# An adaptive-norm router that reads raw rows, and one point of interleaved work moved ahead of the next expert turn's gather

## The reference, cut to what matters

```python
mod = cond @ w_ada + b_ada
shift1, scale1, gate1, shift2, scale2, gate2 = jnp.split(mod, 6, axis=-1)
x = x + gate1[:, None, :] * hybrid_mixer(h, ...)          # 256 x 1024
h = rms_norm(x, norm2_w) * (1 + scale2[:, None, :]) + shift2[:, None, :]
logits = h @ w_router + b_router                          # 256 x 32
top_v, top_e = lax.top_k(logits, 4); gates = softmax(top_v)
# rows of h are sorted by expert; for each expert e in use:
y_e = clamped_swiglu(h[rows_e] @ w1[e] + b1[e]) @ w2[e] + b2[e]
x = x + gate2[:, None, :] * sum over a row's experts of gate * y
```

## Time and profile before

| what | value |
|---|---|
| median of 3 runs (lowest, highest) | 2353.44 us (2350.11, 2357.47) |
| the profiled execution's own time | 2354.66 us |
| its span | 2353.0 us |
| mean granted TensorE clock (share of full speed) | 0.973 |
| busy share: PE, DVE, ACT, POOL | 92%, 59%, 28%, 7% |
| moved by DMA | 713.89 MB, mean 303 GB/s |
| chain that ended last: PE, DMA, DVE, ACT, issue | 67%, 14%, 13%, 2%, 2% |

### The profile page before, as it was taken

One profiled execution on the slowest core, in us unless ns is written; L12 is line 12 of the kernel. 1 busy time (PEld: TensorE's weight loads), 2 busy tenths in 40 slices (PEclk: granted clock), 3 DMA queues, 4 the chain that ended last, 5 costly groups with the idle time before them and its releaser, 6 DMA issues.

```text
span 2353.0 us, 40321 instructions
## 1 busy us (share of the span) xinstructions
PE 2156.2 (92%) x16516; PEld 1507.4 (64%) x16516; DVE 1378.7 (59%) x2660; ACT 659.5 (28%) x832; POOL 170.2 (7%) x229
## 2 busy tenths in 40 slices
PE   6998989988998998888998889899989999998998
PEld 5897843444544445445544555677769888876987
DVE  2466454534453444565544455877678676678876
ACT  1332120212222221211111111444443334455332
POOL 1320010000000000000000000000000000020000
PEclk8999989999999999999999999999999999999999
DMA  9889879998999999999999999554446533334652
GB/s 382 309 324 353 322 294 386 420 419 362 419 419 419 407 420 419 419 410 419 404 419 419 409 404 403 199 174 166 167 145 213 183 137 119 108 117 159 209 187 72
DMA packets 112031, 713.89 MB, mean 303 GB/s; under 512 B 12624, under 2 KB 13280, under 8 KB 36912
## 3 DMA queue, kind: packets, MB, share of 16 engines
q1 hardware_dynamic: 86048, 616.93, 66.4%
q0 software_dynamic: 25808, 94.48, 10.7%
HBM read 705.06 MB, written 4.19 MB: 301 GB/s over the span
## 4 chain that ended last, share of the span: by engine, by line
PE 67%; DMA 14%; DVE 13%; ACT 2%; issue 2%; POOL 0%; SPq 0%; DVEq 0%; ACTq 0%
PE bank L326 17%; PE bank L2366 6%; PE bank L2347 6%; PE bank L2094 4%; PE bank L2132 4%; DMA hT<-in_panels_e 3%; PE bank L2247 3%; DMA cst<-in_panels_e 3%; DMA ring<-in_units_a 2%; PE bank L2295 2%; PE bank L2480 2%; PE bank L1589 2%; DMA hid<-in_panels_e 2%; PE bank L1755 2%; DMA craw<-in_panels_m 2%
## 5 line engine op out<-in xcount | busy, mean ns | idle before, releaser
L326 PE MATMUL bank<-hid,scratch 128*32 128x512 f32 x1008 | 306.3, 606 | 7.8 <-DMA hT<-in_panels_e 4.3
L326 PE MATMUL bank<-hT,scratch 128*32 128x512 f32 x976 | 301.2, 608 | 12.9 <-DMA hT<-in_panels_e 11.5
L1343 ACT CAST chi<-craw 128x1024 fp32r<-128x1024 f32 x128 | 133.7, 1045 | 544.0 <-DMA craw<-in_panels_m 203.7
L3400 DVE TENSOR_TENSOR clo<-craw,chi 128x1024 fp32r<-128x1024 f32 x128 | 156.0, 1221 | 156.1 <-ACT chi L1343 155.1
L326 PE MATMUL bank<-rows,scratch 128*32 128x512 f32 x632 | 172.1, 601 | 8.0 <-DMA cst<-in_panels_e 7.2
L326 PE MATMUL bank<-diag_gtmp,scratch 128*32 128x512 f32 x648 | 177.2, 600 | 2.0 <-DMA hid<-in_panels_e 1.5
L326 PE MATMUL bank<-cst,scratch 128*32 128x512 f32 x632 | 175.6, 603 | 3.0 <-DMA yacc<-in_panels_e 3.0
L326 PE MATMUL bank<-yacc,scratch 128*32 128x512 f32 x648 | 174.0, 595 | 2.5 <-DMA diag_gtmp<-in_panels_e 2.5
L2094 PE MATMUL bank<-cT_hi,chi 128*128 128x256 f32 x384 | 113.3, 295 | 17.2 <-DVE cT_lo L3319 5.5
L326 PEld LDWEIGHTS bank<-hT,scratch 128*32 128x32 f32 x976 | 70.5, 111 | 66.0 <-issue 65.5
L2094 PE MATMUL bank<-cT_lo,chi 128*128 128x256 f32 x384 | 110.3, 287 | 0.0
(11 more groups left out here) (721 smaller groups left out, 5813.5 us busy)
## 6 DMA issues: line engine op xcount, KB each, us to landing
hid<-in_panels_e SPq DMA_DIRECT2D x96, 1024.0 KB, 12.8
hT<-in_panels_e SPq DMA_DIRECT2D x94, 1024.0 KB, 13.4
ring<-in_units_a SPq DMA_DIRECT2D x70, 1024.0 KB, 7.8
ring<-in_panels_m SPq DMA_DIRECT2D x64, 1024.0 KB, 5.1
yacc<-in_panels_e SPq DMA_DIRECT2D x48, 1024.0 KB, 12.4
diag_gtmp<-in_panels_e SPq DMA_DIRECT2D x48, 1024.0 KB, 13.8
rows<-in_panels_e SPq DMA_DIRECT2D x47, 1024.0 KB, 13.1
cst<-in_panels_e SPq DMA_DIRECT2D x47, 1024.0 KB, 12.7
```

The lines of the kernel that those rows point to most:

```text
L326: m = self.pe.matmul(b[s:s + STRIP, :], lhs(k)[:, s:s + STRIP], v, start=(first and k == 0), stop=(k == KT - 1))
L1343: act.copy(chi[:, h % 2, :], context_raw(h)).then_inc(cx_hi, 1)
L3400: tt(context_lower(h), context_raw(h), chi[:, h % 2, :], ALU.subtract).then_inc(cx_lo, 1)
```

## The change

*Raw rows.* The norm's scale is multiplied into the router's weights `wr` and the router's product with the shift is added to its bias `brow`, both while the mixer still runs. TensorE transposes `tok` itself, ScalarE copies the banks out unscaled, and VectorE multiplies the summed logits by `rstd` and adds `brow`. The upper part of the normed rows is made by ScalarE from `tok` and `rstd` (so `xn` is not made), the lower part by VectorE in four pieces (`lower_rows`). *First bias.* Its loads no longer wait for `b1_go`; ScalarE's copy (after `b1_go`) and GpSimd's subtraction come before the router. *First gather.* `first_gather` takes the four products with `xr_hi` first, and turned gates come after the gathered rows; a turn's first product starts after half of the gathered rows, its second half panel after all. *Loads.* One half panel is issued between two ring units, not after the rows are ready. *Turns.* On VectorE `beside(9)` stands ahead of `weights` and `gathered`.

```diff
@@ ScalarE: first bias, rows
-            act.sem_inc(rowp.free, 2)
...
-                    m = act.activation(hT[:, k, t * P:t * P + P], b[:, (k % 4) * P:(k % 4) * P + P], ACT.Identity,
-                                       scale=scol[:, 0, k:k + 1], bias=scol[:, 1, k:k + 1])
...
+            act.wait_ge(filled, B1_FILLED)
+            act.wait_ge(b1_in, 32)
+            act.wait_ge(b1_go, 1)
+            act.copy(b1t[:, :], b1raw).then_inc(b1_upper, 1)
...
+            def row_columns(t, c):
+                act.wait_ge(rows_turned, 2 * t + c + 1)
+                act.copy(hT[:, 4 * c:4 * c + 4, t * P:t * P + P], bank[2 * t + c][:, :].rearrange("p (k n) -> p k n", k=4))\
+                    .then_inc(rows_out, 1)
...
-                act.copy(xr_hi[:, t, :], xn[:, t, :]).then_inc(upper_ready, 1)
+                act.activation(xr_hi[:, t, :], tok[:, t, :], ACT.Copy, scale=rstd[:, t:t + 1]).then_inc(upper_ready, 1)
@@ SyncE
-            for n in range(late + 2, late + 4):
-                first_unit(n, UNIT)
-            first_panel(rows_ready, XT, 1, 0)
+            first_unit(late + 2, UNIT)
+            half_panel(pe_[1], load_of(-1, 1, 1), 1)
+            first_unit(late + 3, UNIT)
+            sp.wait_ge(rows_ready, XT)
+            half_panel(pe_[1], load_of(-1, 1, 0), 0)
@@ GpSimd
-            pool.wait_ge(b1_go, 1)
...
-            for t in range(XT):
-                pool.wait_ge(upper_ready, FRONT_PARTS + t + 1)
-                pool.tensor_tensor(xr_lo[:, t, :], xn[:, t, :], xr_hi[:, t, :], ALU.subtract).then_inc(lower_in, 1)
-            pool.wait_ge(lower_in, FRONT_PARTS + XT)
+            pool.wait_ge(b1_in, 32)
@@ TensorE: shift through the router, ahead of the level chain; into the bias, between two features
+            S.close(partial_sums(b, router, lambda k: scol[:, 1, k:k + 1], range(KT)))
...
+            S.close(pe.matmul(b[:, 0:EXPERTS], shift_part.to_broadcast([P, P]), stack[:, :], start=True, stop=True))
@@ TensorE: router
+            for t in range(XT):
+                for c in range(2):
+                    from_dve.get()
+                    for k in range(4):
+                        m = pe.transpose(bank[2 * t + c][:, k * P:k * P + P], tok_part(t, 4 * c + k), ident)
+                    m.then_inc(rows_turned, 1)
...
@@ TensorE: first gather
+                pieces = [(xr_hi, t, c) for c in range(2) for t in range(XT)]
+                pieces += [(xr_lo, 0, 0), (xr_lo, 0, 1), (xr_lo, 1, 0), (xr_lo, 1, 1)]
...
-            gather()
-            turn_gates()
+            first_gather()
             turn_gathered(0)
             turn_gathered(1)
-            S.read()
+            turn_gates()
@@ TensorE: first product of a turn
-                EA.read()
+                EA.read(1)
@@ VectorE: fold
+            scales(0, 3, {0: (parcol[:, 8:16], None)}, (0,))
...
+            S.done(copy(shift_part, b[:, 0:1]))
+            S.settle()
+            tt(wr[:, :, :], wr[:, :, :], scol[:, 0, :].unsqueeze(2).to_broadcast([P, KT, EXPERTS]), ALU.mult)
...
+            S.done(tt(brow[:, :], brow[:, :], b[:, 0:EXPERTS], ALU.add))
...
@@ VectorE: lower rows, logits
+                stt(xr_lo[:, t, s], tok[:, t, s], rstd[:, t:t + 1], xr_hi[:, t, s], ALU.mult, ALU.subtract).then_inc(lower_in, 1)
...
-                to_tensor.send(ts(xn[:, t, :], tok[:, t, :], rstd[:, t:t + 1], None, ALU.mult))
...
+                m = stt(lg[:, t, :], b[:, EXPERTS * t:EXPERTS * t + EXPERTS], rstd[:, t:t + 1], brow[:, :], ALU.mult, ALU.add)
...
@@ VectorE: an expert turn
                 second(0)
+                beside(9)
                 dve.wait_ge(EA.pair.full, EA.c.at(1))
                 weights(following, shares)
                 gathered(0)
                 gathered(1)
                 if last:
                     added_so_far()
-                beside(9)
```

More of the change, by code:

```diff
@@ L1947, in _ @@
             rows_product(1)
[L1949 to L1961, removed]
-            b = S.open()
[L1963 to L1970, removed]
-            R.read()
-            partial_sums(b, router, cols[1], range(4))
-            S.read()
-            S.close(partial_sums(b, router, cols[1], range(4, KT)))
-            b = S.open()
-            pe.matmul(b[:, 0:EXPERTS], logit_part[:, 0, :], stack[:, :], start=True, stop=True)
-            S.read()
-            S.close(pe.matmul(b[:, EXPERTS:2 * EXPERTS], logit_part[:, 1, :], stack[:, :], start=True, stop=True))
+            for t in range(XT):
[4 more added lines that the diff above has]
+                    m.then_inc(rows_turned, 1)
+            for t in range(XT):
+                b = A.open()
+                for c in range(2):
+                    pe.wait_ge(rows_out, 2 * t + c + 1)
+                    m = partial_sums(b, router, lambda k: hT[:, k, t * P:t * P + P], range(4 * c, 4 * c + 4))
+                A.close(m)
+            b = S.open()
+            for t in range(XT):
+                A.read(XT - 1 - t)
+                m = pe.matmul(b[:, EXPERTS * t:EXPERTS * t + EXPERTS], logit_part[:, t, :], stack[:, :], start=True, stop=True)
+            S.close(m)
             ada_product(AD)
@@ L2007, in _, with first_gather @@
             from_experts = Post(pe, E["to_pe"])
+            def first_gather():
+                pe.wait_ge(upper_ready, FRONT_PARTS + XT)
+                EA.read()
+                pe.wait_ge(EH.pair.free, 2)
+                pieces = [(xr_hi, t, c) for c in range(2) for t in range(XT)]
+                pieces += [(xr_lo, 0, 0), (xr_lo, 0, 1), (xr_lo, 1, 0), (xr_lo, 1, 1)]
+                for n, (piece, t, c) in enumerate(pieces):
+                    if n >= 4:
+                        pe.wait_ge(lower_in, FRONT_PARTS + n - 3)
+                    m = pe.matmul(EH.pair.banks[c][:, :], OH[:, t, :], piece[:, t, 512 * c:512 * c + 512],
+                                  start=(n in (0, 2)), stop=(n >= 6))
+                    if n >= 6:
+                        EH.close(m)
             def gather():
@@ L2030, in first_product @@
                 for h in range(2):
+                    if h and j == 0:
+                        EA.read()
                     EG.rows(b, lambda k: xg[:, k, :], False, h)
@@ L2144, in expert_turn @@
                     pe.wait_ge(b2_in, 16)
+                    S.read()
                     AD.read()
@@ L3076, in _ @@
                     m = gated_rows(c, t)
+                    if t and not c:
+                        lower_rows(0, 0)
                 ask_roots(m, (t,), center=False, eps=EPS_RMS)
                 roots_in((t,))
[L3079 removed]
                 dve.memset(idle[:, 1:2], 0.0).then_inc(rows_ready, 1)
+            for t in range(XT):
+                b = A.take()
+                A.done(copy(logit_part[:, t, :], b[:, 0:P]))
             b = S.take()
[L3082 to L3092 removed]
+            for t in range(XT):
+                m = stt(lg[:, t, :], b[:, EXPERTS * t:EXPERTS * t + EXPERTS], rstd[:, t:t + 1], brow[:, :], ALU.mult, ALU.add)
+            S.done(m)
             S.settle()
```

60 lines of the change are left out of this document (27 added, 33 removed).

## The result

The changed kernel takes 2342.89 us (median of 9 runs, 2335.81 to 2351.32) against 2353.44 (9 runs, 2350.11 to 2359.65): ratio 0.9941, 95% interval 0.9928 to 0.9954, so about 14 us less with 11 and 17 as bounds. The ratio is the one on record and is not that of the two medians, which differ by 10.6 us (0.9955); the two means differ by 12.0. The gain is therefore known to a few microseconds only. The forecast was 2341, within 2335 to 2349, a gain of 12.7. The profiled execution has a span of 2339.7.

A forecast was written before the change was run, and what follows sets the result against it. The cross-engine chain before the first expert product, then the weight stream, bound the kernel. Start 7.3, turn 1 3.9 and turn 9 1.5 sum to 12.7 us, from 2354.66 (2342.0) or median 2353.44 (2340.7): 2341, range 2335 to 2349.

The forecast's parts named there:

- A: From the end of the mixer's output product to the router's logits: 10.5 us becomes 5.8, gain 4.7.
- B: From the logits to VectorE's read of the counts: gain 3.2 us, with GpSimd's subtraction moved away and the counts ending last.
- E: From the first gather matmul to the first expert product: 7.04 us becomes 5.5 to 5.6, gain 1.5.
- the pair: VectorE's two 128x32 gate-scaling instructions, 4.46 us before, would fall to near 0.5 once clear of GpSimd's subtraction.
- Ahead of T0: Before the mixer's output product ends (T0): norm scale and shift folded into the router cost 2.1 us, 0.8 to 2.6.
- C: From the read of the counts to the one-hots and first gather matmul: unchanged at 2.47 us.
- Rival 4: TensorE's low clock through router and gather gives 2343.3, or GpSimd's moved subtraction 2346.5; chance 0.66 shared with the sum.
- D: Lower halves of the normed rows: four VectorE subtractions replace GpSimd's two, covered by upper gather matmuls to within 0.2 us.
- rival 1: Weight stream takes the earlier start back, with panel waits up to 380 us: 2349.3, or 2348 by the median; chance 0.12.
- The tenth point: Expert turns, VectorE's crot_lo made ahead of next turn's rows: gain 3.9 us in turn 1, 1.5 in turn 9.
- Rival 2: In turn 1 the wait at the tenth point only moves and stays as long: 2345.9 us; chance 0.12.
- Rival 3: Next turn's gathered rows come late at turn ends, so TensorE waits: slower, 2365 us; chance 0.06.

The follow-up runs named there:

- the changed kernel once more: The changed kernel measured a second time without any edit: ratio 0.9926 (0.9904 to 0.9947), median 2342.40 us.
- the full read: Changed kernel with a turn's first product waiting again for all eight gathered-row instructions: 2350.39 us, one time only.
- both points ahead: Changed kernel with the eleventh point ahead of one-hots and gathered rows and the fourth ahead of the places for the next experts: ratio 0.9928.
- the later start: Changed kernel with ten repeats of one lower-rows operation on VectorE ahead of the one-hots, changing no value: ratio 0.9978 (0.9964 to 0.9992).
- the first bias late: Changed kernel with ScalarE's first-bias copy, and so GpSimd's subtraction, back behind the exponentials: ratio 0.9950 (0.9931 to 0.9968).
- the tenth point alone: Kernel before with only `beside(9)` moved ahead of the next turn's one-hots and gathered rows: ratio 0.9976 (0.9962 to 0.9991).
- the eleventh point ahead: Changed kernel with `beside(10)` too moved ahead of the one-hots and gathered rows: 2351.99 us in one execution; also run with the fourth point moved, ratio 0.9928.
- the front alone: Changed kernel with the tenth point put back behind the one-hots and gathered rows: ratio 0.9961 (0.9948 to 0.9975).

## Why the prediction was right

The mechanisms of the sum came as forecast: the chain became shorter by the terms A, B and E, the pair was freed, the earlier start was carried to the end, and turn 1's wait was halved. Of the signs that the prediction names, the pair (0.39 for 0.5) and turn 1's wait (3.75 for 3.6) fit; the first product, at 16.98 and 16.1 after T0, came earlier than 18 to 19.5, and the clock behind it did not stay as it was. The terms one by one:

**Ahead of T0: forecast +2.1, measured +1.76.** T0 itself can't tell, since it lies between 308.19 and 314.71 in the ten profiles, with neighbouring values for kernels with and without the fold (308.64 with, 308.67 without). The local intervals can. On VectorE, from the copy of the modulation row ahead of the fold to the delta rule's multiply (220.28 in the earlier trace rows), the kernel before begins at

```profile
217.81 0.29 DVE L2646 COPY arow<-bank 128x128 f32<-128x128 f32 x1 [1.42 <-PE bank L1589]
```

and the changed kernel has

```profile
216.51 0.29 DVE L2650 COPY arow<-bank 128x128 f32<-128x128 f32 x1 [1.42 <-PE bank L1585]
...
217.12 0.17 DVE L2689 TENSOR_TENSOR scol<-scol,parcol 128x8 f32<-128x8 f32 x1
...
219.76 0.16 DVE L3004 COPY xn<-bank 128x1 f32<-128x1 f32 x1
219.95 0.42 DVE L3006 TENSOR_TENSOR smallw<-smallw,scol 128x256 f32<-128x256 f32 x1
220.29 1.22 DVE L3007 TENSOR_TENSOR scratch<-scratch,dnw 128x1024 f32<-128x1024 f32 x1
```

That is 2.47 before and 3.78 after, so 1.31 for the fold (2.48 in the other kernel without it, 3.77 to 3.84 in the other seven with it). From that multiply to T0 it is 89.26 in both kernels without and 89.61 to 89.71 in those with the bias's add: 0.4, as forecast. In the first profile the front happened to reach the fold 1.30 earlier, which hid most of this.

**A: forecast 4.7, measured 5.7** (10.52 to 4.83 from T0 to the logits). The term was mis-sized in its last step. To the end of the router's partial sums the forecast was 3.3 and the trace has 3.26 (313.26); the two copies, the stack matmuls and the two small operations behind them took 1.57 where the sum had 2.5. The bounds 5.4 and 6.4 of that paragraph are of the new length, not of the gain, and 4.83 lies below both. **B: 3.2, measured 3.8** (7.94 to 4.15). The mechanism was right: the collision is gone, and the counts end last. They begin 2.74 after the logits (317.57), released by VectorE's picks after 1.31 of idle time; the modulation product ahead of them, which the forecast took to hold them, ran at the high clock and was out of the way. **C: 0, measured -0.6** (2.47 to 3.04). Rival 4 had the lower clock in A, B and E; it came here. The second modulation product, 64 matmuls, took 3.28 us at a granted clock of 0.57, mostly the lower level of 1.2 GHz (318.80 on), and ended at 322.08, after the first one-hots were there; the gather stood behind it. In the three other profiles of the new front in which it took 1.95 us and the gather followed the one-hots at once (the changed kernel once more, the full read, both points ahead), C is 2.48, as forecast. **D: 0, as forecast**: the lower gather matmuls (323.33) follow the upper ones without a gap. **E: 1.5, measured 2.1** (7.04 to 4.96), of which 1.27 is the half read.

Together 11.0 less 1.8, 9.2 for a forecast of 7.3, just above its bound of 9; in the second profile of the changed kernel 11.9 less 1.8, 10.1.

**Does it carry? Yes.** The first wait of TensorE for a panel of more than half a microsecond is the same one in both kernels, of the same length, before:

```profile
491.10 0.62 PE L326 MATMUL bank<-yacc,scratch 128*32 128x512 f32 x2 [1.26 <-DMA diag_gtmp<-in_panels_e]
```

and after:

```profile
483.54 0.62 PE L326 MATMUL bank<-yacc,scratch 128*32 128x512 f32 x2 [1.26 <-DMA diag_gtmp<-in_panels_e]
```

It came 7.56 earlier. Ahead of it stands only a wait for the half panel before, 0.33 at 482.05 before and 0.10 at 474.51 after; rival 1 wanted waits up to 380. It is refuted for these profiles, and the later start confirms it from the other side. But 3.2 of the first profile's 10.5 were given back between 336 and 399 us, and not to the stream. The table by stretch for the second and third interval between first products, before:

```profile
346.90:357.90 11.00, 9.92 (x72) 2.96 (x71) 3.67 (x8) 0.00 (x0) 0.00 (x0) 1.00 0.95 381
357.90:367.30 9.40, 9.40 (x69) 2.75 (x69) 2.29 (x11) 0.00 (x0) 0.76 (x1) 0.82 0.94 390
```

after:

```profile
336.30:348.10 11.80, 10.72 (x72) 3.04 (x71) 3.67 (x8) 0.00 (x0) 0.00 (x0) 0.93 1.01 417
348.10:358.50 10.40, 10.40 (x71) 2.99 (x70) 2.34 (x11) 0.00 (x0) 0.78 (x2) 0.75 0.82 338
```

TensorE did the same work in 11.80 + 10.40 in place of 11.00 + 9.40 at a granted clock of 0.93 and 0.75, against 1.00 and 0.82. The kernel with the first bias late is like before here:

```profile
342.30:353.40 11.10, 10.02 (x73) 3.06 (x72) 3.66 (x8) 0.00 (x0) 0.00 (x0) 1.00 0.94 387
353.40:362.90 9.50, 9.50 (x71) 2.89 (x70) 2.33 (x11) 0.00 (x0) 0.78 (x2) 0.82 0.92 383
```

The later start, which began its first product at nearly the same time (334.10, against 332.97), was like the changed kernel (0.92 and 0.76, 12.00 and 10.15). So it isn't how early the turn begins that decides. All ten profiles fall into two groups: the second and third interval take 20.5 to 20.6 us together in the three kernels with the first bias in its old place (before, the tenth point alone, the bias late), and 22.1 to 22.2 in the other seven. The kernel with the bias late differs from the changed kernel in nothing else, so the earlier subtraction, which gives 4.5 us at the start, goes with a loss of 1.6 here; this may be why that kernel's ratio is only 2 us above. By what way the bias's place reaches TensorE's clock, through the instruction itself or through the moments at which TensorE works and waits ahead of the stretch, stays open. A second dip in the fifth interval (0.86 or 0.87, about 1.4 us) is in the changed kernel both times, in the one with the bias late and in the one with the full read, and larger with the eleventh point ahead (0.76, 3.0 us); it is in neither the front alone, nor the tenth point alone, nor the later start. So in these profiles it appears only where both parts of the change stand together, the loss that their times could not show; it too is unexplained.

**The tenth point: forecast 3.9 + 1.5, measured 5.7 (2 to 9) alone.** The waits of TensorE in the changed kernel at turns 1 and 9, which answer to the earlier trace rows:

```profile
542.78 0.80 PE L2137 MATMUL bank<-chi,crot_hi 128*128 128x512 f32 x1 [3.75 <-DVE crot_lo L3376]
...
1348.68 0.50 PE L2137 MATMUL bank<-chi,crot_hi 128*128 128x512 f32 x1
...
1352.84 0.50 PE L2137 MATMUL bank<-chi,crot_hi 128*128 128x512 f32 x1 [1.10 <-DVE clo L3413]
```

Turn 1's wait went from 7.64 to 3.75, 3.89 less. In turn 9 the first product of the piece, at 1348.68, has no wait (2.03 before), but the eleventh point then waits 1.10 for clo, which VectorE now makes after the gathered rows: 0.9 net where 1.5 stood. The other turns were put at nothing. That fails in turn 2, where the eleventh point now waits for its crot_lo, made behind the gathered rows, and had no such wait before (677.24):

```profile
667.61 0.50 PE L2137 MATMUL bank<-chi,crot_hi 128*128 128x512 f32 x1 [1.78 <-DVE crot_lo L3376]
```

It is absent from the front alone and from the kernels with the eleventh point ahead, so the tenth point's move made it. What it costs isn't shown: it lies where the stream sets the pace (1.01), and TensorE's waits for panels near it changed as well. Rival 2, that turn 1's wait only moves and turn 9's 1.5 is all that is left, is refuted by the tenth point alone: its gain is 5.7, and the lower bound, 2, is just above 1.5. Rival 3 did not come; with the eleventh point ahead it does. The DMA engines restarted earlier, as forecast: 0.78 in the 13 us around turn 1's tenth point.

So the sum of 12.7 came from a start 1.9 too small, a clock loss that it did not have, and a tenth point within its interval; its agreement with 14, or with the medians' 10.6, is closer than its terms, and that part is luck. The range held all of it; the upper end given for the likeliest case, 2345, does not follow from its own terms, which give up to 2348 (2353.44 less 5.5 and 2, with 2 added). What the first profile shows of the terms, 9.2 - 3.2 + 3.9 + 0.9 = 10.8, is the lower bound of the measured interval; up to 3 us beside it are assigned to nothing. From the first product to 1500 us, TensorE's waits for panels sum to 36.1 us before and 34.0 after, but to between 31.4 and 38.7 in the other eight profiles, so this difference isn't shown to belong to the change.

## What to carry to other kernels

In a chain that passes between engines, count for each step which engine's result ends last and what stands ahead of it in that engine's own queue: here an unrelated GpSimd instruction held VectorE for 4 us, and work for the next turn stood ahead of the result that TensorE waited for. An earlier start ahead of a stream-bound stretch was carried to the end here, where the stream had stood still behind it (a DMA share of 0.43); look for such a low share before counting on it. Moving one point ahead paid and moving the next gave back as much, above all at the last turn, where other work was pushed into TensorE's way; so the margin to the next use has to be read anew for each, at the ends of the loop too.

## What the runs showed of the hardware

The granted clock of TensorE repeated between the two profiles of the changed kernel in three stretches (0.93 and 0.94, 0.75 and 0.74, 0.87 and 0.87) and not in a fourth: the second modulation product took 3.28 us at 0.57 in one and 1.95 at 1.00 in the other. It differs between kernels that do the same work: from the second to the fifth interval the changed kernel lost 3.3 us to it against the kernel before, the front alone, the bias late and the later start 1.7, and the two kernels with the eleventh point ahead 4.9. The front's length varies from execution to execution by up to 6.5 us (T0 from 308.19 to 314.71 in ten profiles), more than most terms of this change. It varies ahead of the fold: from the fold's multiply to T0 it is 89.61 to 89.71 in the eight profiles of the new front.
